# Gathering expert tokens with the choice as stationary operand, longer dummy runs in two waits, and a last pass and final norm by token tile

## The reference

```python
def moe_swiglu(h, router_w, router_b, w_gate, w_up, w_down):
    t = h.reshape(B * S, D)                                  # 256 x 1024
    logits = t @ router_w + router_b                         # 8 experts
    top_v, top_i = lax.top_k(logits, 2)
    gates = jax.nn.softmax(top_v, axis=-1)
    combine = sum(one_hot(top_i, 8) * gates[..., None], axis=1)
    for e in range(8):
        out = out + combine[:, e:e + 1] * swiglu(t, w_gate[e], w_up[e], w_down[e])   # width 3584
x = x + moe_swiglu(rmsnorm(x), ...)
return rmsnorm(x, final_norm_g)
```

## Time and profile before

| | |
|---|---|
| three runs | 1460.54, 1461.05, 1462.93 us |
| profiled execution | 1459.61 us |
| its span in the trace | 1457.8 us |
| mean granted TensorE clock | 0.992 |
| read from HBM | 414.95 MB, 286 GB/s over the span |
| busy: TensorE, VectorE, ScalarE, GpSimd | 98%, 80%, 67%, 4% |

### The profile page before, as it was taken

The page is one execution under the profiler, slowest core; times in us unless marked ns, Lnnn a source line. Parts: engine busy times, 40 slices in busy tenths (PEclk is TensorE's granted clock), DMA queues, the critical chain, the costliest instruction groups (busy, mean ns, idle before and its releaser), DMA issues.

```text
span 1457.8 us, 21728 instructions
## 1 busy us (share of the span) xinstructions
PE 1427.9 (98%) x7413; PEld 1208.4 (83%) x7413; DVE 1171.7 (80%) x1319; ACT 972.2 (67%) x1179; POOL 64.2 (4%) x108
## 2 busy tenths in 40 slices
PE   8999999999899999999999999999999999999996
PEld 7886899998878888888888888888888888888885
DVE  2793354456667998998999899899989989989996
ACT  1045343445655877877887877788878778878884
POOL 1060000002230000000000000000000000000000
PEclk9999999999998999999999999999999999999999
DMA  9500655555534999999899899999989999999991
GB/s 291 199 30 9 223 189 187 191 185 173 166 124 145 378 358 338 350 370 387 314 374 370 322 367 362 339 359 363 385 311 379 358 338 363 356 380 322 374 372 56
DMA packets 193776, 417.49 MB, mean 286 GB/s; under 512 B 6879, under 2 KB 43871, under 8 KB 193726
## 3 DMA queue, kind: packets, MB, share of 16 engines
q1 hardware_dynamic: 192222, 412.79, 79.2%
q0 software_dynamic: 1344, 3.98, 1.2%
q10 hardware_dynamic: 160, 0.04, 0.0%
HBM read 414.95 MB, written 1.84 MB: 286 GB/s over the span
## 4 chain that ended last, share of the span: by engine, by line
PE 94%; DVE 2%; ACT 2%; issue 1%; POOL 1%; DMA 0%; ACTq 0%; POOLq 0%; DVEq 0%
PE bank L960 78%; PE bank L901 4%; PE bank L924 3%; PE bank L1164 2%; PE bank L947 2%; PE bank L1203 2%; PE bank L1215 1%; DVE wl L1383 1%; ACT prob L723 1%; PE bank L868 1%; POOL prob L554 0%; DMA R<-in_conv_ln_b 0%; PE bank L856 0%; ACT wh L661 0%; DVE prob L1473 0%
## 5 line engine op out<-in xcount | busy, mean ns | idle before, releaser
L1383 DVE TENSOR_TENSOR wl<-ring,wh 128x1024 fp32r<-128x1024 f32 x758 | 910.9, 1229 | 107.4 <-ACT wh L661 68.7
L661 ACT CAST wh<-ring 128x1024 fp32r<-128x1024 f32 x758 | 788.7, 1054 | 191.8 <-PE bank L960 191.3
L960 PE MATMUL bank<-wh,low 128*128 128x512 f32 (+1 forms) x1840 | 577.0, 393 | 1.2 <-DVE wl L1383 1.1
L960 PEld LDWEIGHTS bank<-wh,low 128*128 128x128 f32 x1840 | 341.6, 189 | 71.3 <-DVE wl L1383 4.1
L960 PE MATMUL bank<-wl,low 128*128 128x512 f32 x896 | 350.1, 391 | 0.0
L960 PE MATMUL bank<-wh,ath 128*128 128x512 f32 x528 | 206.1, 390 | 0.0
L960 PE MATMUL bank<-wl,ath 128*128 128x512 f32 x528 | 205.6, 389 | 0.0
L960 PE MATMUL bank<-wh,atl 128*128 128x512 f32 x528 | 205.6, 389 | 0.0
L960 PEld LDWEIGHTS bank<-wl,low 128*128 128x128 f32 x896 | 168.5, 188 | 36.2
L960 PEld LDWEIGHTS bank<-wl,ath 128*128 128x128 f32 x528 | 99.1, 188 | 20.8
L960 PEld LDWEIGHTS bank<-wh,atl 128*128 128x128 f32 x528 | 99.2, 188 | 20.0
(11 more groups left out here) (211 smaller groups left out, 1160.3 us busy)
## 6 DMA issues: line engine op xcount, KB each, us to landing
ring<-in_moe_w_gate SPq DMA_DIRECT2D x112, 1024.0 KB, 6.6
ring<-in_moe_w_up SPq DMA_DIRECT2D x112, 1024.0 KB, 6.9
ring<-in_moe_w_down SPq DMA_DIRECT2D x112, 1024.0 KB, 6.9
ring<-in_conv_pw_w SPq DMA_DIRECT2D x12, 1024.0 KB, 10.8
ring<-in_ffd_w_gate SPq DMA_DIRECT2D x11, 1024.0 KB, 5.4
ring<-in_ffd_w_up SPq DMA_DIRECT2D x11, 1024.0 KB, 5.3
ring<-in_ffd_w_down SPq DMA_DIRECT2D x11, 1024.0 KB, 4.9
ring<-in_w_q SPq DMA_DIRECT2D x4, 1024.0 KB, 5.4
```

The lines of the kernel that those rows point to most:

```text
L661: sa.copy(wh[:, place(n, h), :], ring_half(n, h)).then_inc(wh_ready, 1)
L960: mm = pe.matmul(out_bank, lhs, rhs, start=start and n == 0, stop=stop and n == 2, **kw)
L1383: ve.tensor_tensor(wl[:, place(n, h), :], ring_half(n, h), wh[:, place(n, h), :].bitcast(F32), ALU.subtract).then_inc(wl_ready, 1)
```

## The change

1. `gather` makes rows first: `pick` is the stationary operand and 512 features of `hnh` or `hnl` the moving one, eight products, with tokens on the partitions, in banks 5 and 6. ScalarE copies the two banks to the new tile `xg_rows` (`take_rows`), and TensorE transposes it in eight blocks of 128 (`gather_T`) back into banks 5 and 6.
2. The last block's `expert_out` is cut in two, with `gather_T` between its parts. ScalarE copies the first "d" unit ahead of `act_high` and the second behind `take_rows`; VectorE does likewise around `act_low`.
3. `keep_busy` issues 17 instead of 12 products ahead of the parameters and 11 instead of 6 ahead of the mask.
4. In the last pass `combine(i, 1)` writes banks 0 and 1 and doesn't wait for the additions of the first tile.
5. `x_final` is raised per token tile, so that the first tile's squares start while the second is added. The scaling and the store of a tile go in halves of 512 features.

```diff
@@ -120,6 +120,7 @@
...
         gate_slot = sb("gate_slot", [P, 1])
+        xg_rows = sb("xg_rows", [P, D])
         qh = sb("qh", [P, DC, S], F32R)
...
@@ -290,6 +291,8 @@
...
         slots_ready = sem("slots_ready")
+        rows_done = sem("rows_done")
+        rows_ready = sem("rows_ready")
         gathered = sem("gathered")
...
@@ -464,10 +467,12 @@
...
             for t in range(TT):
-                sp.wait_ge(final_ready, t + 1)
-                sp.dma_start(out[0, t * P:(t + 1) * P, :], X[:, t, :]).then_inc(stored, 16)
-            sp.wait_ge(stored, 16 * TT)
+                for half in range(2):
+                    cols = slice(half * HALF, (half + 1) * HALF)
+                    sp.wait_ge(final_ready, 2 * t + half + 1)
+                    sp.dma_start(out[0, t * P:(t + 1) * P, cols], X[:, t, cols]).then_inc(stored, 16)
+            sp.wait_ge(stored, 16 * 2 * TT)
...
@@ -773,6 +778,12 @@
...
+            def take_rows(i):
+                for half in range(2):
+                    sa.wait_ge(rows_done, 2 * i + half + 1)
+                    sa.copy(xg_rows[:, half * HALF:(half + 1) * HALF], PB[5 + half][:, :]).then_inc(rows_ready, 1)
             def take_xg(i):
...
@@ -813,8 +824,10 @@
...
                     split_high(i, "d", b - 1)
+                high_parts(expert_at["d", EB - 1, 0], i)
                 act_high(i, EB - 1)
-                split_high(i, "d", EB - 1)
+                take_rows(i + 1)
+                high_parts(expert_at["d", EB - 1, 1], i)
                 take_xg(i + 1)
...
@@ -825,6 +838,7 @@
...
+            take_rows(0)
             take_xg(0)
...
@@ -835,7 +849,7 @@
...
-                sa.wait_ge(x_final, 1)
+                sa.wait_ge(x_final, t + 1)
                 sa.activation(R1[:, t * D:(t + 1) * D], X[:, t, :], ACT.Square,
...
@@ -856,7 +870,7 @@
...
             pe.wait_ge(consts, 6)
-            keep_busy(1, 12)
+            keep_busy(1, 17)
             pe.wait_ge(params_in, 16 * 7)
...
@@ -1142,7 +1156,7 @@
...
                 mm.then_inc(logits_done, 1)
-            keep_busy(3, 6)
+            keep_busy(3, 11)
...
@@ -1156,13 +1170,21 @@
...
                 pe.wait_ge(slots_ready, i + 1)
+                for half in range(2):
+                    for t in range(TT):
+                        for n, part in enumerate((hnh, hnl)):
+                            mm = pe.matmul(PB[5 + half][:, :], pick[:, t, :],
+                                           part[:, t, half * HALF:(half + 1) * HALF],
+                                           start=(t == 0 and n == 0), stop=(t == 1 and n == 1))
+                    mm.then_inc(rows_done, 1)
+            def gather_T(i):
                 for q in range(2):
+                    pe.wait_ge(rows_ready, 2 * i + q + 1)
                     for k in range(4):
                         ch = (4 * q + k) * P
-                        for t in range(TT):
-                            for n, part in enumerate((hnh, hnl)):
-                                mm = pe.matmul(PB[5 + q][:, k * P:(k + 1) * P], part[:, t, ch:ch + P], pick[:, t, :],
-                                               start=(t == 0 and n == 0), stop=(t == 1 and n == 1))
+                        mm = pe.transpose(PB[5 + q][:, k * P:(k + 1) * P], xg_rows[:, ch:ch + P], ident[:, :])
                     mm.then_inc(gathered, 1)
...
@@ -1183,10 +1205,10 @@
...
-            def expert_out(i, b):
+            def expert_out(i, b, parts_of=range(2)):
                 pe.wait_ge(atl_ready, i * EB + (b + 1))
-                for part in range(2):
+                for part in parts_of:
                     n = expert_at["d", b, part]
...
@@ -1203,16 +1225,16 @@
...
-            def combine(i, t):
+            def combine(i, t, banks=(5, 6)):
...
                         pe.wait_ge(y_low, 2 * i + (half + 1))
-                    else:
+                    elif banks[0] == 5:
...
                     for n, part in enumerate((yh, yl)):
-                        mm = pe.matmul(PB[5 + half][:, :], placeT[:, t * P:(t + 1) * P],
+                        mm = pe.matmul(PB[banks[half]][:, :], placeT[:, t * P:(t + 1) * P],
                                        part[:, half * HALF:(half + 1) * HALF], start=(n == 0), stop=(n == 1))
...
@@ -1232,18 +1254,23 @@
...
                 gather(i + 1)
-                expert_out(i, EB - 1)
+                expert_out(i, EB - 1, (0,))
+                gather_T(i + 1)
+                expert_out(i, EB - 1, (1,))
...
                     expert_in(i + 1, "u", 0)
-                combine(i, 1)
+                    combine(i, 1)
+                else:
+                    combine(i, 1, (0, 1))
...
             gather(0)
+            gather_T(0)
...
@@ -1640,12 +1667,12 @@
...
-            def add_share(i, t):
+            def add_share(i, t, banks=(5, 6)):
...
                     xs = X[:, t, half * HALF:(half + 1) * HALF]
-                    ve.tensor_tensor(xs, PB[5 + half][:, :], xs, ALU.add).then_inc(o_added, 1)
+                    ve.tensor_tensor(xs, PB[banks[half]][:, :], xs, ALU.add).then_inc(o_added, 1)
...
@@ -1664,8 +1691,9 @@
...
                         slots(i + 1)
+                low_parts(expert_at["d", EB - 1, 0], i)
                 act_low(i, EB - 1)
-                split_low(i, "d", EB - 1)
+                low_parts(expert_at["d", EB - 1, 1], i)
                 take_xg(i + 1)
...
@@ -1679,9 +1707,13 @@
...
                 add_share(i, 0)
-                if not last:
+                if last:
+                    ve.wait_ge(o_added, i * 4 + 2)
+                    ve.nop().then_inc(x_final, 1)
+                    add_share(i, 1, (0, 1))
+                else:
                     split_low(i + 1, "g", 1)
-                add_share(i, 1)
+                    add_share(i, 1)
...
@@ -1690,13 +1722,22 @@
...
             ve.nop().then_inc(x_final, 1)
-            for t in range(TT):
-                mean_square(4, t)
+            def final_scale(t, half):
+                cols = slice(half * HALF, (half + 1) * HALF)
+                root_done(4, t)
+                ve.scalar_tensor_tensor(out=X[:, t, cols], in0=X[:, t, cols], scalar=rstd[:, 4, t:t + 1],
+                                        in1=gF[:, cols], op0=ALU.mult, op1=ALU.mult).then_inc(final_ready, 1)
             ve.wait_ge(gf_in, 16)
-            for t in range(TT):
-                root_done(4, t)
-                ve.scalar_tensor_tensor(out=X[:, t, :], in0=X[:, t, :], scalar=rstd[:, 4, t:t + 1], in1=gF,
-                                        op0=ALU.mult, op1=ALU.mult).then_inc(final_ready, 1)
+            mean_square(4, 0)
+            final_scale(0, 0)
+            mean_square(4, 1)
+            root_done(4, 1)
+            final_scale(0, 1)
+            final_scale(1, 0)
+            final_scale(1, 1)
...
```

## The result

The changed kernel took 1450.14 us (median of four runs, 1449.07 to 1451.2) against 1461.37 for the kernel before (four runs). The ratio of the two is 0.9934 with a 95% interval of 0.9916 to 0.9952; with more runs in a second comparison 0.9923 (0.9910 to 0.9937). It is faster, beyond the 0.2% that can be told, and the forecast 1448.8 was 1.3 us short of it. The profiled executions took 1459.61 and 1450.40 (spans 1457.8 and 1448.7), so they differ by 9.2 us where the forecast's sum was 12.25. The hit on the median is therefore in part luck, as shown further down.

The account below looks back on a forecast made before the run. TensorE's own time was taken to bound the passes. Terms 3.3 + 0.8 + 4.4 + 1.95 + 1.8 = 12.25 took the profiled 1459.61 to 1447.4; adding 1.44 for the median gave 1448.8 us, range 1446 to 1454.

Parts of the forecast that it names:

- head, first norm: Kernel start: ten more dummy records keep the clock up, the first norm's 32 products take 3.52 instead of 5.47: 1.95 us.
- start of the expert stage: First gather: at full clock it takes 1.83 instead of 6.91 us, and the whole path behind moves: 4.4 us.
- seven boundaries: Between passes: each gather saves 0.81 us, a TensorE wait for the first weights costs 0.33; net 0.48, in all 3.3.
- last gather: Last pass: only the result follows the down block, so the gather there gives its full 0.8 us.
- tail: Final norm and stores: earlier squares, a 0.55 us second power operation, half scalings and half stores save 1.8 us.
- They cost nothing while the clock is full: Ahead of the mask: ten added dummy records, 1.10 us, end at 442.5 against the wait's end at 442.6.
- rival (a): Clock does not hold at head, first gather or both: 1450.8, 1452.1 or 1454.1 us; chance 0.30.
- The worry that ten more records could outlast the parameters: Head: at the slow pace the dummies end at 9.8, 0.5 us past the parameters; taken to end before 9.29.
- The choice taken for the power operation: Tail: the second one's 1.54 us is the VectorE scaling's doing and becomes 0.55; otherwise 1.0 of the 1.8 is lost.
- (b): Passes: transfers are the bound behind TensorE, passes stay at 123.8 and the 3.3 is lost: 1452.1 us; chance 0.08.
- (c): Pass boundaries: the wait does not come, all of 0.81 us is kept in seven boundaries: 1446.4 us; chance 0.10.
- (d): Each pass: the earlier down-block weight copy waits for its load, queueing others behind it; slower, 1467.4 us; chance 0.02.

Follow-up runs that it names:

- early_gate: Changed kernel with the first half of the next pass's first gate weights split before the gathered tokens are taken: 1447.20 us, against 1449.45 for the changed kernel.
- no_cut: Changed kernel without the cut of the last down block, the row transposes directly behind the gather: 1449.53 us.
- early_again: early_gate run once more, unaltered: 1447.19 us, ratio 0.9914 to the kernel before.
- the two wide ones: Two runs of early_gate with the router's product records at 128 moving columns instead of 8: 1446.07 and 1446.94 us.
- no_dummies: Changed kernel with 12 and 6 dummy products again instead of 17 and 11: 1452.83 us, against 1449.45 for the changed kernel.
- gather_only: Kernel before with only the gather by rows, its row copies and the cut of the last down block: 1455.19 us, ratio 0.9964.
- before: The kernel before the change, unaltered: 1461.37 us (median of four runs).
- before_wide: Kernel before with only the router's product records widened from 8 to 128 moving columns: 1459.77 us, ratio 0.9997.
- after_again: The changed kernel run again, unaltered, for a second profile: 1449.45 us (five runs).
- early_mask8: early_gate with 8 instead of 11 dummy products ahead of the routing mask: 1447.81 us, against 1447.20 for early_gate.
- norm_order: Changed kernel with the second token tile's mean ahead of the first scaling on VectorE: 1450.35 us (four runs).
- whole_stores: Changed kernel with each token tile stored in one piece of 512 KB when its second half is scaled: 1451.31 us.

## Why the prediction was right, and where its sizes were off

The direction, the mechanism and the time came out; the single terms less so, and the time is closer than they deserve. The sum was 3.1 us too large, so the profiled execution took 1450.40 where 1447.4 was forecast. The forecast then added 1.44, by which the median lay above the profiled execution before. In the kernel after, the median lies 0.26 below it, and this makes up for 1.7 of the 3.0. That part is luck: the size of the gain in the median, 11.2, is nearer to the forecast than what the traces of the pair account for.

The profiled pair, stretch by stretch (before less after, us):

| term | forecast | measured | where the difference went |
|---|---|---|---|
| head, first norm | 1.95 | 2.06 | 1.63 from the products; 0.44 because the parameters landed earlier in that execution |
| attention | 0 | -0.36 | a bias load was waited for in this execution; over the profiles this stretch varies by 1.0 |
| start of the expert stage | 4.4 | 2.91 | below |
| seven boundaries | 3.3 | 2.51 | below |
| last gather | 0.8 | 0.86 | |
| tail | 1.8 | 1.12 | below |
| sum | 12.25 | 9.1 | |

**Gather.** 32 x 0.110 became 8 x 0.230 and 8 x 0.112: 2.74, as forecast (2.71).

**Boundary.** The forecast put the first gate product 8.96 behind the activation's transposes; it came at 695.45 - 686.46 = 8.99. The wait itself is 0.36 (forecast 0.33). `early_gate` shows that it is the helper path: one weight half moved in front of the takes, the wait is gone, and a pass is 0.75 shorter than before, of the 0.81 that the gather saves. The term was mis-sized by what follows a wait: the first products after it are farther apart (0.73 for two records in place of 0.62), some 0.08 in all, so that a pass gave 0.36 and not 0.48. The wait for the row copies cost nothing, as forecast, but `no_cut` shows that hiding it did not earn anything either: the idle moves from the transposes to the gate weights.

**Start of the stage.** The step that failed is "They cost nothing while the clock is full", said of the dummies ahead of the mask. It was given as a condition, and rival (a) took its breach to cost 3.3 us at this place. What the runs showed is a third way: the clock fell, but in the dummies, and it was back for the gather. They stuck 1.47 us out of the wait (forecast for this case 1.0), and the gather started 12.14 behind the router's transposes instead of 10.88. The first half of the first gate block ended 5.41 us after the gather's start, against 9.59 before: 4.18 of the 4.4. Less the 1.26 of the later start that is 2.9. In the profiles where the clock did not fall (`no_cut`, `early_again` and the two wide ones) the stretch to the first pass is 27.6 against 31.67: 4.1. So the fall cost 1.2, and even without it the 4.4 was 0.3 too high.

The profiled pair alone looks as if the added dummies had moved the fall forward. The other profiles do not bear that out: with six dummies the clock fell ahead of the mask, too, in `no_dummies` (440.4) and `gather_only` (439.5). What goes with the number of dummies is how long the clock row then reads 0.50: 10.2 us in `before`, `before_wide` and `no_dummies` and 6.8 in `gather_only`, all with six; 3.4 in the six profiles with eight or eleven in which it fell. The idle of 1.17 us was not the last thing before the fall either: in the kernel before it ended at 442.62, and the clock fell at 444.7, behind ten records of 8 columns and eight more of dummies.

**Head.** Right in mechanism. All ten profiles with 17 dummies ran the first norm at 1.00, and all four with twelve read 0.50 for 3 us or more of it. The worry that ten more records could outlast the parameters did not come true in the profiled execution: 34 records took 5.61 us, where 24 had taken 5.49, so the pace rose while they ran, though the clock row reads 1.00 throughout. In `after_again` and `early_mask8` TensorE did not wait for the parameters at all, so there the dummies may have outlasted them; the first norm began at 9.24 and 9.42, against 9.67.

**Transposes.** By the Trainium skill ("TensorE: Matmul & The Clock Gate", Part 4) transposes do not count as activity in the way products do. They did no harm behind the gather: the clock held through both groups in every profile in which it was up before them.

**Tail.** The first square started 2.23 behind the first combining product (forecast 2.16), the second 3.94 (forecast 3.56, 3.72 in `after_again` at full clock). The fall of the clock in the combining products took 0.2 to 0.3 of the 1.8 (11.04 against 10.73 to 10.82 for the same stretch at full clock). The rest went in small parts: 0.16 in the second square's start, 0.1 from there to the second root, 0.12 in the three half scalings (they end 2.12 after the second root, forecast 2.0), 0.06 in the store. The choice taken for the power operation was right: 0.55 when VectorE waits for it. The price of that order is that the mean of the second tile stands behind the first scaling and starts at 1443.23, though its square was done at 1442.75; `norm_order` shows that nothing is to be gained by turning it round, since the power operation is then longer by as much. The Trainium skill ("SBUF — State Buffer", who interferes with whom) describes such a lock, and the trace agrees: the operation's end follows the scaling's by 0.40 at either length. The half store gave 0.54 between the profiled pair and 0.57 in `whole_stores` (forecast 0.6).

**Rivals.** (a) came in part, as told. (b), transfers as the bound, is out: passes went down to 123.05 with the same 42 units of weights each. (c) did not come by itself, but `early_gate` brought it about, with 1447.2 for the 1446.4 it was given. (d) did not come: no weight copy waited for a load.

**Left open.** Why the clock falls around the mask in some executions and not in others, and why it is back after 3.4 us with eight or eleven dummies and only after 6.8 or 10.2 with six. No profile of the 14 departs from this split, but the runs do not say what decides.

## What to carry to other kernels

When the engine that bounds a kernel gets faster, read the slack of the helper path at its next meeting point before counting the gain: here a path with only 0.3 us of cover took away half of 0.8 us per pass, and moving one weight copy in front of it gave it back. A block that is split to hide a new step is worth measuring unsplit as well: the idle that the split hides can come back at the next wait. Dummy products in a wait are priced at both clocks, since at the low one they can outlast the wait that was to hide them. And a pair of profiles is not enough to say what moved a fall of the clock: here two more profiles of kernels without the added dummies had it in the same place.

## What the runs showed of the hardware

- Six, eight or eleven dummy products ahead of the same wait did not prevent a fall of the granted clock. With six it read 0.50 for 6.8 or 10.2 us (four profiles of four), with eight or eleven for 3.4 us (six of ten) or not at all (four of ten).
- Executions of one kernel differ in how long the clock is low: the kernel before took 1453.61 to 1463.81 over more than 40 runs, the changed one 1448.42 to 1451.2 in nine. In the kernel before the time and the mean granted clock go together: 0.993 to 0.994 in the five executions that took 1453.6 to 1455.8, 0.985 to 0.992 in the others. Where the clock was up in those five was not profiled.
- A 128-column float32 record and an 8-column one take nearly the same time on TensorE when each has its own weight load: 32 in 3.74 and 3.64 us.
- A GpSimd power operation of 128 x 1 elements takes 0.55 us, and ends 0.40 us after a VectorE scaling with two SBUF inputs that it runs into (0.98 and 1.54 us).
